# Reordering the hand-written schedule of a two-layer hybrid decoder: one PSUM bank pair fewer in the input projection, retention moved ahead of the last attention scores

## The reference, cut to what matters

```
x = x + 1/2 * SwiGLU_1(RMSNorm(x))
z = RMSNorm(x) @ w_in              # 2944 columns: u | q k v (attention) | q k v gate (retention)
A = causal mean pooling of u, 4 groups of 64
B = 6 heads of attention; the sample group attends to 1024 cached keys (blocks of 256, the best 3 of
    4 past blocks by mean key) and to its own 8
C = 6 heads of retention (decay mask), normalised per head by the mean square, times silu(gate)
x = x + concat(A, B, C) @ w_out
x = x + 1/2 * SwiGLU_2(RMSNorm(x))
```

## Time and profile before

| | |
|---|---|
| median of 3 runs | 1402.97 us (1401.73 to 1403.62) |
| the profiled execution: its own time | 1403.62 us |
| its span in the trace | 1401.9 us |
| PE busy | 1338.4 us, 95% of the span |
| PE weight loads | 1285.9 us, 92% |
| DVE, ACT, POOL busy | 795.9 us (57%), 652.4 us (47%), 251.3 us (18%) |
| chain that ended last | PE 81%, issue 10%, DVE 2%, POOL's queue 2%, DMA 2% |
| HBM to core and back | 235.28 MB, 168 GB/s over the span |

### The profile page before, as it was taken

The page is one execution under the profiler, slowest core; times in us unless marked ns, Lnnn a source line. Parts: engine busy times, 40 slices in busy tenths (PEclk is TensorE's granted clock), DMA queues, the critical chain, the costliest instruction groups (busy, mean ns, idle before and its releaser), DMA issues.

```text
span 1401.9 us, 28364 instructions
## 1 busy us (share of the span) xinstructions
PE 1338.4 (95%) x11129; PEld 1285.9 (92%) x11129; DVE 795.9 (57%) x878; ACT 652.4 (47%) x717; POOL 251.3 (18%) x352
## 2 busy tenths in 40 slices
PE   5999999999977999999999999999997799999998
PEld 4999999999756999999999999999984689999998
DVE  4555545569753655554555555546885555555554
ACT  3655543334434555553455554333431646555434
POOL 3000000365552100000100000015645510000001
PEclk9999999999999999999999999999998899999998
DMA  6444544867876444444444445467767934444443
GB/s 191 154 149 147 173 153 157 216 179 196 194 230 226 151 150 150 150 143 141 165 141 148 148 147 166 154 190 198 209 154 186 339 122 146 148 147 149 144 139 124
DMA packets 210928, 235.28 MB, mean 168 GB/s; under 512 B 15006, under 2 KB 203176, under 8 KB 210836
## 3 DMA queue, kind: packets, MB, share of 16 engines
q1 hardware_dynamic: 200828, 204.90, 48.0%
q0 software_dynamic: 9888, 29.14, 6.7%
q10 hardware_dynamic: 120, 0.03, 0.0%
HBM read 228.83 MB, written 5.32 MB: 167 GB/s over the span
## 4 chain that ended last, share of the span: by engine, by line
PE 81%; issue 10%; DVE 2%; POOLq 2%; DMA 2%; POOL 1%; ACT 1%; DVEq 0%; SPq 0%; ACTq 0%
PE ps L1244 21%; PE ps L1245 21%; PE ps L1246 21%; PE ps L1326 3%; PE ps L1328 3%; PE ps L1327 3%; PE ps L1469 2%; PE ps L1506 1%; DVE w_lo L865 1%; PE ps L1640 1%; POOLq L567 1%; DMA v_c<-in_cache_v 1%; PE ps L1642 1%; PE ps L1641 1%; POOLq L287 1%
## 5 line engine op out<-in xcount | busy, mean ns | idle before, releaser
L606 ACT ACTIVATE w_hi<-w_raw 128x2048 fp32r<-128x2048 f32 x170 | 325.6, 1915 | 537.3 <-PE ps L1246 424.0
L865 DVE TENSOR_TENSOR w_lo<-w_raw,w_hi 128x2048 fp32r<-128x2048 f32 x162 | 371.3, 2292 | 211.1 <-ACT w_hi L606 208.4
L1244 PE MATMUL ps<-h_hi,w_hi 128*128 128x320 f32 x768 | 240.3, 313 | 10.2 <-DVE w_lo L865 3.5
L1245 PE MATMUL ps<-h_lo,w_hi 128*128 128x320 f32 x768 | 239.0, 311 | 0.0
L1246 PE MATMUL ps<-h_hi,w_lo 128*128 128x320 f32 x768 | 238.8, 311 | 0.0
L1244 PE MATMUL ps<-g_hi,w_hi 128*128 128x320 f32 x704 | 218.4, 310 | 1.2 <-DVE g_lo L872 1.2
L1246 PE MATMUL ps<-g_hi,w_lo 128*128 128x320 f32 x704 | 217.7, 309 | 0.0
L1245 PE MATMUL ps<-g_lo,w_hi 128*128 128x320 f32 x704 | 217.7, 309 | 0.0
L1245 PE MATMUL ps<-act_lo,w_hi 128*128 128x320 f32 x704 | 217.5, 309 | 0.0
L1244 PE MATMUL ps<-act_hi,w_hi 128*128 128x320 f32 x704 | 217.5, 309 | 0.0
L1246 PE MATMUL ps<-act_hi,w_lo 128*128 128x320 f32 x704 | 217.5, 309 | 0.0
(11 more groups left out here) (283 smaller groups left out, 1922.9 us busy)
## 6 DMA issues: line engine op xcount, KB each, us to landing
w_raw<-in_ffn_w_in SPq DMA_DIRECT2D x90, 1024.0 KB, 5.1
w_raw<-in_ffn_w_out SPq DMA_DIRECT2D x32, 896.0 KB, 4.6
kbuf<-in_cache_k SPq DMA_DIRECT2D x128, 192.0 KB, 5.0
w_raw<-in_w_in SPq DMA_DIRECT2D x22, 1024.0 KB, 5.6
w_raw<-in_ffn_w_out SPq DMA_DIRECT2D x16, 1024.0 KB, 4.9
kbuf<-in_cache_v POOLq DMA_DIRECT2D x48, 192.0 KB, 4.6
w_raw<-in_w_out SPq DMA_DIRECT2D x8, 1024.0 KB, 11.7
v_c<-in_cache_v POOLq DMA_DIRECT2D x32, 192.0 KB, 8.4
```

Source lines behind the costliest of these rows:

```text
L606: act.activation(w_hi[:, slot, :], w_raw[:, slot, :], ACT.Copy).then_inc(hi_done, 1)
L865: dve.tensor_tensor(w_lo[:, slot, :], w_raw[:, slot, :], w_hi[:, slot, :].bitcast(F32), ALU.subtract).then_inc(split_done, 1)
L1244: pe.matmul(out, w_hi[:, slot, w], hi[:, k, :], start=(k == 0), stop=False)
L1245: pe.matmul(out, w_hi[:, slot, w], lo[:, k, :], start=False, stop=False)
```

## The change

Eight edits, none of which adds or removes a matmul, a DMA or an elementwise operation:

1. `mix(1)` uses PSUM banks 0 and 1 like all other chunks, and waits for the evacuation of chunk 0 there.
2. PE runs `ret_out(1)` and `smp_state(1)` ahead of `sample_scores(3)` (they stood behind it), then `ret_out(2)` and `smp_state(2)`, and `mean_squares()` ahead of `transpose_probs(0)` (it stood behind `transpose_probs(1)`).
3. DVE spreads `decay_mask(4)` and `decay_mask(5)` between the last `turn_k`, runs `soft_in(3)` ahead of `new_state(2)`, and groups `or_norm` and `or_lo`.
4. ACT runs `exps(2)` ahead of `ret_square(2)`, `root_o` ahead of `probs_evac(0)`, and `exps(3)` right behind it; `or_high` all three in one place.
5. The homes of V for u = 5 and u = 6 are swapped, and `load_v_all(5)` now waits for `transpose_probs(1)` and the last `spread_v` user, not for `smp_out(0, 0)`.
6. `load_v_all(1)` waits for `mix(11)`, where it waited for `mix(10)`.
7. w_out's first two squares are loaded in the other order, slot 1 first.
8. `transpose_out` of the first three pairs goes to bank 4 instead of bank 5; the wait for `root_o` moves ahead of it.

```diff
-        V_HOME = "CXWABCDA"
+        V_HOME = "CXWABDCA"
...
-                for slot, cols in enumerate((slice(0, 256), slice(256, 512))):
-                    wait_apart(sp_e, pv_done, NB * L + 2 + slot)
-                    square(A["w_out"], L, half0 + C_WO // 2, cols, slot, apart=True)
+                wait_apart(sp_e, pv_done, NB * L + 2)
+                square(A["w_out"], L, half0 + C_WO // 2, slice(256, 512), 1, apart=True)
+                wait_apart(sp_e, pv_done, NB * L + 3)
+                square(A["w_out"], L, half0 + C_WO // 2, slice(0, 256), 0, apart=True)
...
-                wait_apart(pool, chunk_used, L * C_ALL + (C_MIX + 13))
+                wait_apart(pool, chunk_used, L * C_ALL + (C_MIX + 14))
                 load_v_all(1)
-                wait_apart(pool, chunk_used, L * C_ALL + (C_MIX + 14))
                 load_v_all(2)
...
-                wait_apart(pool, pv_done, NB * L + 1)
-                load_v_all(5)
                 wait_apart(pool, vbd_used, H * L + H)
                 wait_apart(pool, pt2_done, NB * L + 4)
-                load_v_all(6)
-                wait_apart(pool, pv_done, NB * L + 4)
-                load_v_all(7)
+                load_v_all(5)
+                for u, n in ((6, 1), (7, 4)):
+                    wait_apart(pool, pv_done, NB * L + n)
+                    load_v_all(u)
...
-                for f in range(3):
-                    ret_square(f)
+                ret_square(0)
+                ret_square(1)
+                exps(2)
+                ret_square(2)
                 act.wait_ge(sp_done, L + 1)
                 act.activation(sp_new[:], ps[:, 6, 320:512].rearrange("p (f v) -> p f v", f=3), ACT.Copy).then_inc(st_prm, 1)
+                for f in range(3):
+                    root_o(f)
                 probs_evac(0)
-                exps(2)
+                exps(3)
...
-                    dve.tensor_tensor(z[:, 2 * c, :], ps[:, 2 if c == 1 else 0, 0:TOK], rstd[:], ALU.mult).then_inc(mix_half, 1)
+                    dve.tensor_tensor(z[:, 2 * c, :], ps[:, 0, 0:TOK], rstd[:], ALU.mult).then_inc(mix_half, 1)
...
                 gate(2)
+                soft_in(3)
                 new_state(2)
-                soft_in(3)
...
-                        if c < 2:
+                        if c == 0:
                             banks_free(L, G_MIX)
                         elif a == 0:
                             pe.wait_ge(mix_half, L * 11 + c)
...
-                sample_scores(3)
                 ret_out(1)
                 smp_state(1)
+                sample_scores(3)
                 ret_out(2)
+                smp_state(2)
+                wait_apart(pe, sm_in, L * 4 + 4)
+                mean_squares()
                 wait_apart(pe, r_mask, H * L + 6)
                 transpose_probs(0)
-                smp_state(2)
```

More of the change, by code:

```diff
@@ L247, in build @@
         v_landed = {n: sem("v_landed_" + n) for n in "CWXABD"}
-        V_HOME = "CXWABCDA"
+        V_HOME = "CWXABDCA"
         q_own = sem("q_own")
@@ L281, in o_smp @@
         def o_smp(half, p):
-            rows = ps[HD * half:HD * half + HD, 5 if p < 3 else 1, 8 * half:8 * half + 224].rearrange("p (b n) -> p b n", b=2)
+            rows = ps[HD * half:HD * half + HD, 4 if p < 3 else 1, 8 * half:8 * half + 224].rearrange("p (b n) -> p b n", b=2)
             return rows[:, :, 0:96].rearrange("p b (f x) -> p b f x", f=3)[:, :, :, 0:8]
@@ L817, in _ @@
                 for f in range(3):
-                    root_o(f)
+                    or_high(f)
                 out_evac(1, 0)
@@ L822, in _ @@
                 probs_evac(2)
-                exps(3)
                 out_evac(2, 0)
                 y_high(1)
-                or_high(0)
                 mix_hi(12)
@@ L829, in _ @@
                 probs_evac(3)
-                or_high(1)
-                or_high(2)
                 out_evac(3, 0)
@@ L958, in evac_last @@
                     b = 1 if c < 11 else 0
-                    dve.tensor_tensor(z[:, 2 * c + b, :], ps[:, b + (2 if c == 1 else 0), 0:TOK], rstd[:], ALU.mult).then_inc(evac_done, 1)
+                    dve.tensor_tensor(z[:, 2 * c + b, :], ps[:, b, 0:TOK], rstd[:], ALU.mult).then_inc(evac_done, 1)
                 def mix_lo(c):
@@ L1161, in _ @@
                 gate(0)
+                decay_mask(4)
                 turn_k(3, 1, 0)
                 new_state(0)
+                decay_mask(5)
                 turn_k(3, 1, 1)
-                decay_mask(4)
-                decay_mask(5)
                 gate(1)
@@ L1193, in y_rest @@
                     ins.then_inc(ys_low, 1)
-                or_norm(0)
+                for f in range(3):
+                    or_norm(f)
+                for f in range(3):
+                    or_lo(f)
+                soft_sum(3)
                 y_rest(0)
-                or_norm(1)
-                or_norm(2)
-                soft_sum(3)
                 y_rest(1)
@@ L1203, in _ @@
                 mix_lo(12)
-                for f in range(3):
-                    or_lo(f)
                 y_rest(2)
@@ L1324, in mix @@
                             w = slice((k * (2 if c < 11 else 1) + a) * P, (k * (2 if c < 11 else 1) + a + 1) * P)
-                            out = ps[:, a + (2 if c == 1 else 0), 0:TOK]
+                            out = ps[:, a, 0:TOK]
                             pe.matmul(out, w_hi[:, c % 2, w], h_hi[:, k, :], start=(k == 0), stop=False)
@@ L1513, in transpose_out @@
                         wait_apart(pe, o_evac, L * NB + p * 2 + (bb + 1))
-                        ins = pe.transpose(ps[:, 5 if p < 3 else 1, 96 * bb:96 * bb + 96], o_tok[p % 2][:, bb, :], ident[0:96, 0:96])
+                        ins = pe.transpose(ps[:, 4 if p < 3 else 1, 96 * bb:96 * bb + 96], o_tok[p % 2][:, bb, :], ident[0:96, 0:96])
                     ins.then_inc(ot_done, 1)
@@ L1627, in _ @@
                 transpose_probs(1)
-                wait_apart(pe, sm_in, L * 4 + 4)
-                mean_squares()
                 smp_out(1, 0)
+                wait_apart(pe, o_std, 3 * L + 3)
                 transpose_out(0)
```

2 lines of the change are left out of this document (removed).

## The result

The changed kernel takes 1418.51 us (median of 4 runs, 1416.15 to 1420.14) against 1402.35: ratio 1.0112, 95% interval 1.0095 to 1.0131. It is slower, outside the range that was given; a second set of runs on another occasion gave 1.0111 (1.0088 to 1.0133). The profiled execution took 1416.02 us, its span 1414.3, mean granted clock 0.977 (before 0.982).

What follows compares the result with a forecast made beforehand. PE, busy 95% of the span, was taken to bound the kernel. Gap +4.8, clock +3.4, end of the stage -6.2 gave +2.0 us: 1405.6 on the profiled execution, 1405.0 against the median; range 1398.5 to 1411.

Steps and rivals of the forecast that it cites:

- Part 1: Ahead of mix(1): PE waits for evac_first(0), 2.4 us a layer; half clock behind it costs 1.7 (0 to 2.7).
- Part 2: load_v_all(1) waits for mix(11): POOL's first DMA at 371.0, its work 1.7 us later.
- Part 3: Retention fills PE's wait for keys: keys ready at 392.5, own scores over at 397.1, smp_out(0, 0) 0.9 us sooner.
- Part 4: Value pages: u = 3 and 4 issued from 395 to 406.5, u = 5 from 411.9, there at about 423.5.
- No DMA rest at 395: Sign to look for in the mixing stage: the DMA engines' rest, 9 GB/s from 395 to 400 before, is gone.
- Part 5: w_out's slot 0, issued at 414.1, lands at 427.5; first product at 434.9, gaining 1.3 and 4.9 us.
- rival (a): Slot 0 lands late, each microsecond past 427.5 counting twice; at 430.5 total +8 to +10 us; chance 0.25.
- the end of the stage: Term for the end of mixing, up to the first product with w_out: 6.2 us gained over both layers.
- The 439.8 for layer 1: Layer 1's first product with w_out before the change, 1119.10, put on layer 0's clock by taking off 679.3 us.
- rival (b): SP's queue gets an even share, slot 0 lands at 424.5: 11 us gained, 1397 to 1400 us; chance 0.18.

Runs made afterwards that it cites:

- f3: Changed kernel with four dense 128x320 matmuls in PE's wait ahead of smp_state(0), nothing else: ratio 1.0077 to the kernel before.
- e3: Changed kernel with the homes of V for u = 1 and 2 as before and w_out's slot 0 loaded first: ratio 1.0047.
- e4: e3 with load_v_all(1) waiting for mix(10) again, as before the change: 1406.31 us, ratio 1.0017.
- e9: e4 with mix(1) in banks 2 and 3 again: ratio 0.9973.
- e1: Changed kernel with mix(1) back in banks 2 and 3, nothing else undone: 1410.46 us, ratio 1.0033.
- f2: Kernel before with mix(1) in banks 0 and 1, plus 22 dense matmuls in PE's wait ahead of mix(1): ratio 1.0058, again 1.0059.
- f1: e3 with four dense 128x320 matmuls in PE's wait ahead of smp_state(0): ratio 1.0027.

## Why the prediction was wrong, step by step

**Part 1 was right.** 2.4 us of wait and 1.7 of clock a layer, 8.2 together; A grew by 8.6. In layer 1 the clock's part was 2.4 to 2.8, near the upper end given. (The row with 0.62 puts the clock's return at 397.8 and not at 397.6, a tenth of a microsecond a layer.)

**Part 2 is where it failed.** POOL's first page went at 371.5 on the clock of before (371.0 predicted). The step then said: "Nothing waits for this but `smp_state(0)` and, now, `smp_state(1)`." That PE itself stands for smp_state(0) was written down and not costed: its wait of 0.76 us became 2.81. The prediction asked about the clock at the gap of mix(1), and did not ask here, in a gap nearly as long with lighter work behind it. The clock fell, and retention's matmuls went at half for 13 us in the layer shown and 10 in the other three.

**Part 3: the order of events was right, each time late.** On the clock of before, with the predicted value in brackets: smp_state(1) 393.7 (390.8), own scores over 401.4 (397.1), smp_out(0, 0) 409.9 (405.6). The keys were not the reason: the last of their loads was issued at 376.9 and none took over 13.9 us, so they were there by 390.8, 389.1 on the clock of before. DVE turned the last of them only from 394.31 to 396.07, 394.4 on that clock where I had 392.5, because edit 3 put decay_mask(4) and decay_mask(5) between the last turn_k, and these wait for PE's scores (DVE idle 5.38 us ahead of the first). PE came to the keys at 397.32 and did not wait. The 4.3 us of lateness are the clock in the main: f3 takes 2.9 of them back with four dense matmuls, and 1.5 where the clock fell later. The 2.33 us ahead of mean_squares are another gap whose clock the step did not ask about; here it held.

**Part 4** inherits it: u = 3 is issued at 400.3 (395) and u = 5 at 416.5 (411.9). So the rest of the DMA engines did not go, as "No DMA rest at 395" asked: they move 19 GB/s from 396 to 400 and nothing from 400 to 402.

**Part 5: the mechanism was right, and so was the time of the load.** Slot 0 took 14.1 us from issue to landing, where the step had 13.4; but it was issued at 419.0 (414.1), so it landed at 433.1 (427.5), and the first product came at 440.2 (434.9). That is rival (a), "slot 0 lands late", 2.6 us beyond its bound of 430.5. Its rule, each microsecond twice, gives 2.0 + 2 * 5.6 = 13.2 us, near the 12.7 of A and B. In this design each microsecond that the stage is late passes through slot 0, since SP can issue it only after smp_out(1, 0). With slot 0 first (e3) it landed 6 us before it was needed. So the term of the sum that was mis-sized is the end of the stage: -6.2 predicted, +4.1 measured (+2.9 in the second profile). The sum by the measured terms is 8.6 + 4.1 = 12.7, against 2.0. Without w_out's order and POOL's wait (e4, e9) B is 4.6 and 5.2 us under the kernel before, close to the 6.2 that were forecast, and e9's time is 0.27% under it. (The 439.8 for layer 1 starts from a row of the chain; the first product itself starts at 1118.88, 0.2 us sooner.)

What rival (b) rests on did not occur: slot 0 didn't land early. In the rows above, SP's queue had close to half of the bytes until 429.0 (0.95 MB beside 1.13) and almost none after it (0.10 beside 2.05); over both together a quarter. The 100 GB/s with which the step reckoned were the mean of one load of the kernel before; this one kept no steady rate. Nor does even mean even in bytes: from 422.8 to 434.8 the two queues moved about as many packets, 1040 and 1032, but of 1.0 KB and 3.1 KB. The Trainium skill (DMA: Bandwidth & Descriptors, section Queues, rings and completion order) states that a DMA engine takes its turns between queues packet by packet; the prediction had read this as halves of the stream. The totals fit turns by packet, if the profile's packets are those of the page, but the course over the 12 us does not, and why the last tenth came so slowly is open.

Left open: the ratio of the changed kernel (1.12%, 15.7 us) is 3 to 4 us more than A and B of its profiles hold, and it fell further in e1 than A did. In the second profile 2.2 us of it lie between the first product with w_out in layer 0 and the sum of squares in layer 1 (513.4 us against 511.2), a stretch that spreads from 511.2 to 514.7 over the kernels other than f2; and both profiled executions were faster than the median of their kernel, by 2.5 and 2.3 us.

## What to carry to other kernels

Where a change delays a queue, look at every engine that waits for it for a microsecond already: its wait grows by the whole delay (2.05 us for 2.2 here), and light work behind it may run at half clock for long (10 to 13 us here), while every row calls the engine busy. Ask of each wait whether the work behind it is what sets the end; in the kernel before the same delay was a gain. And of two loads in one queue beside another queue's stream, the one that is needed first goes first: what counts is when its last packets land, not its mean rate.

## What the runs showed of the hardware that was not expected

- The granted clock fell to half and stayed there for 13 us (PE busy without a pause from 386.7 to 399.9) with the matmuls of retention and scores in the rows above; for some 10.2 us in the other three layers of the changed kernel's two profiles. Four dense 128x320 matmuls, 2.42 us, in the wait ahead put the fall off from 388.3 in e3 (0.58 in the stretch 388 to 390) to 395.2 in f1 (0.81 in 394 to 396).
- The start of one queue's stream 2.2 us later against the stage (5.6 us behind the own scores of page set 2 and not 3.4) shortened the slowest load of another queue by 3.9 us (17.2 to 13.3) and 4.3 us (18.5 to 14.2).
- A 1 MB load in SP's queue beside POOL's pages had moved 0.95 MB in 6.2 us, and the rest took 5.8 us. The packets of SP's queue were 1.0 KB, those of POOL's 3.1 KB.
- Twenty-two more matmuls in the loop of the layers (f2) went with a wait at the seam of the layers of 3.2 us in place of 1.3 to 1.8, in both its traces.
